# RWKV's last tile: the output projection in the scan's stage, its products behind the last scan step

## The reference, cut to what matters

```python
def rwkv_out(y, p, kvec, lnx, w_o):
    r, k, v, g = p["r"], p["k"], p["v"], p["g"]
    y = head_layernorm(from_heads(y), lnx[0], lnx[1], RW_HEADS, r.dtype)
    bonus = jnp.sum((r * k * kvec[2]).reshape(bn, L, RW_HEADS, RW_HEAD), axis=-1, keepdims=True) * v.reshape(...)
    return ((y + bonus.reshape(bn, L, D)) * g) @ w_o
...
        xl = xl + mod_l[2] * rmsnorm(yl, norm_g[layer, 1])          # yl is rwkv_out of the latents
        hl = modulate(rmsnorm(xl, norm_g[layer, 2]), mod_l[3], mod_l[4])
        xl = xl + mod_l[5] * rmsnorm(conv_ffn(hl, ...), norm_g[layer, 3])
```

## Time and profile before

| | us |
|---|---|
| median of 3 executions | 3187.83 (3187.26 to 3189.34) |
| the profiled execution | 3187.58 |
| its span, first to last instruction | 3185.6 |
| PE busy | 3038.0 (95%) |
| DVE busy | 1141.0 (36%) |
| ACT busy | 586.1 (18%) |

### The profile page before, as it was taken

How to read it: one execution, slowest core, us unless ns; L and a number is a source line. 1 busy time by engine, 2 the same in 40 slices (tenths; PEclk the granted TensorE clock), 3 DMA queues, 4 the chain that set the end, 5 groups by cost and what they waited for, 6 DMA issues and landing times. The chain is left out here.

```text
span 3185.6 us, 54300 instructions
## 1 busy us (share of the span) xinstructions
PE 3038.0 (95%) x24038; PEld 1843.0 (58%) x24038; DVE 1141.0 (36%) x2357; ACT 586.1 (18%) x1323; POOL 231.7 (7%) x202
## 2 busy tenths in 40 slices
PE   7999999899999999989987999999999799998998
PEld 5899884633333333344666544444464688887887
DVE  3455006301100111034055444431141778874650
ACT  1011013300000000022045110000021455542000
POOL 0000000100000000000022100000000233230000
PEclk9999999899999999989988999999999899998999
DMA  9846538589998899942000342333321100005440
GB/s 379 315 173 228 202 140 362 223 327 390 387 369 363 332 388 384 397 170 74 14 3 10 150 157 79 119 132 119 123 78 40 43 24 27 16 4 199 146 146 14
DMA packets 88492, 577.03 MB, mean 181 GB/s; under 512 B 9536, under 2 KB 15936, under 8 KB 20672
## 3 DMA queue, kind: packets, MB, share of 16 engines
q1 hardware_dynamic: 84800, 568.27, 45.9%
q10 hardware_dynamic: 3456, 5.24, 0.4%
HBM read 567.19 MB, written 6.29 MB: 180 GB/s over the span
## 5 line engine op out<-in xcount | busy, mean ns | idle before, releaser
L273 PE MATMUL ps<-H,ring 128*128 128x256 f32 (+1 forms) x2480 | 803.8, 486 | 12.6 <-PEq L3297 4.1
L273 PEld LDWEIGHTS ps<-H,ring 128*128 128x128 f32 x2480 | 477.9, 194 | 336.5 <-issue 296.3
L273 PE MATMUL ps<-W,ring 128*128 128x256 f32 (+1 forms) x1616 | 490.5, 465 | 9.1 <-DVE W L3144 4.1
L1963 PE MATMUL ps<-ring,W 128*32 128x512 f32 (+1 forms) x2816 | 461.4, 594 | 1.7 <-ACT H L2022 1.7
L273 PEld LDWEIGHTS ps<-W,ring 128*128 128x128 f32 x1616 | 307.1, 191 | 192.1 <-issue 166.8
L1963 PEld LDWEIGHTS ps<-ring,W 128*32 128x32 f32 (+1 forms) x2816 | 142.5, 123 | 306.6 <-issue 304.0
L1986 PE MATMUL ps<-ring,W 128*64 128x512 f32 (+1 forms) x1408 | 231.1, 594 | 0.0
L2253 DVE SCALAR_TENSOR_TENSOR W<-ps,vec,W 128x189 f32<-128x189 f32 (+3 forms) x396 | 173.2, 437 | 14.0
L1986 PEld LDWEIGHTS ps<-ring,W 128*64 128x64 f32 (+1 forms) x1408 | 70.9, 123 | 156.9 <-issue 156.9
L3728 POOL TENSOR_TENSOR ring<-ring 128x512 f32<-128x512 f32 x96 | 132.6, 1402 | 391.8 <-DVE ring L3761 310.1
L2071 DVE TENSOR_TENSOR H<-ps,H 128x256 f32<-128x256 f32 x66 | 28.0, 425 | 303.2 <-ACT H L2013 303.2
(11 more groups left out here) (468 smaller groups left out, 3172.9 us busy)
## 6 DMA issues: line engine op xcount, KB each, us to landing
ring<-weights SPq DMA_DIRECT2D x528, 1024.0 KB, 7.8
rkv<-W ACTq DMA_DIRECT2D x16, 256.0 KB, 2.0
ring<-rkv SPq DMA_DIRECT2D x8, 512.0 KB, 4.3
X<-tokens SPq DMA_DIRECT2D x2, 1024.0 KB, 9.2
rkv<-W ACTq DMA_DIRECT2D x8, 128.0 KB, 5.5
W<-rw_tiles SPq DMA_DIRECT2D x4, 256.0 KB, 2.7
ring<-rkv SPq DMA_DIRECT2D x8, 128.0 KB, 4.3
ring<-rw_tiles SPq DMA_DIRECT2D x4, 256.0 KB, 2.8
```

The source lines that it names most:

```text
L273: mm = pe.matmul(out(o), lhsT=k.ring[:, k.slot(at), p * P:(p + 1) * P], rhs=rhs(kk), start=kk == 0 and not (shared_bank and o % 2), stop=k ...
L1963: mm = pe.matmul(ps[at:at + n, r, :], lhsT=moe.Hg[:, kt, FIRST * e + first:FIRST * e + first + n], rhs=w[e][:, kk * WIDE:(kk + 1) * WIDE], ...
```

## The change

The output projection moves into the scan's stage. `stage_square` keeps its form for its other uses, with its DVE and ACT parts taken out into a class `Square`. In `stage_rwkv` the loop ends with j = 7 and the last tile's steps are written out behind it, for each engine:

- PE does the eight steps. `output_mean` and `output_squares` of tile 6 come behind steps 0 and 2 (the squares' sum came in step 6). Inside the steps there are places for products, with a count of 0. Behind `last_y`: the mean of tile 7, three products, the squares' sum of tile 7, the rest of the 36 products of outputs 0 to 5 with H tiles 0 to 5, the six with H tile 6, output 6 with tiles 0 to 6, outputs 0 to 6 with H tile 7, and output 7 with all. PE waits for `fin` and for the weight units as it comes to them. Two outputs share a PSUM bank; all eight stay in banks 2, 0, 1 and 3 until they are finished.
- ACT evicts outputs in the same order, each when both outputs of its bank are done.
- DVE does the gate and `finished_output(5)` ahead of the first state update, `output_difference(6)` behind the first, `finished_output(6)` behind the last, then tile 7's, and then the crosses.
- The sum of squares of tiles 6 and 7 goes to bank 7's second half, so step 4 waits for tile 6's root instead of its difference.
- POOL adds the squares at the end of its part of this stage.
- SP issues the first four units when tile 7's transposes, exponentials and query products are done, the other seven behind `wt_out` as before, and then the four refills. The scan's buffers in the ring are in another order, so that those used latest lie outside these four slots.

```diff
+class Square:
+    def vector(self, dve):
+        k = self.k
+        link = Link(k.dvel, dve)
+        for o in range(KD - 1):
+            dve.wait_ge(k.act.sem, k.act.at(o + 1))
+            self.rms.cross(dve, link, o, self.Y)
+        link.close()
+
+    def scalar(self, act, out, done=lambda o: o):
+        k = self.k
+        for o in range(8):
+            act.wait_ge(k.mm.sem, k.mm.at(self.out_done[done(o)]))
+            self.rms.square(act, o, out(o))
+            self.gate.out(act, self.Y, o, out(o)).then_inc(k.act.sem, 1)
...
+    squares_of = lambda q: ps[:, 2 if q < TILES - 2 else sc.Y, S:2 * S]
+    product = lambda o: ps[:, (2, 0, 1, 3)[o // 2], (o % 2) * S:(o % 2) * S + S]
...
-            sp.wait_ge(sem["wt_out"], 2 * TILES)
+            for name, n in (("tok", 6), ("exp", 8), ("vtok", 1), ("r", 1), ("gram_r", 1)):
+                sp.wait_ge(sem[name], n * TILES)
             for u in range(RING):
+                if u == U_SQ:
+                    sp.wait_ge(sem["wt_out"], 2 * TILES)
                 sp.dma_start(k.ring[:, k.slot(u), :], k.a["weights"][k.unit + u]).then_inc(k.w_in[k.slot(u)], 16)
+            refill(k, sp, square.unit_done, U_SQ)
...
-                        pe.wait_ge(sem["d"], s)
+                        pe.wait_ge(sem["d" if s < TILES - 1 else "root_d"], s)
...
-            for j in range(TILES + 2):
+            for j in range(TILES):
...
+            def products(places):
+                for o, kk in places:
+                    u, p = divmod(KD * o + kk, UT)
+                    if u not in landed:
+                        landed.add(u)
+                        pe.wait_ge(k.w_in[k.slot(u)], k.landed(u))
+                    if finished[0] <= kk:
+                        finished[0] = kk + 1
+                        pe.wait_ge(sem["fin"], kk + 1)
+                    mm = pe.matmul(product(o), lhsT=k.ring[:, k.slot(u), p * P:(p + 1) * P], rhs=k.H[:, kk, LAT],
+                                   start=kk == 0 and o % 2 == 0, stop=kk == last, skip_group_check=True)
+                    if kk == last:
+                        mm.then_inc(k.mm.sem, 1)
+
+            early = [(o, kk) for o in range(6) for kk in range(last - 1)]
+            for i in range(8):
+                step_a(last, i)
+                products(early[:0])
+                early = early[0:]
+                step_b(last, i)
+                if i == 0:
+                    output_mean(last - 1)
+                elif i == 2:
+                    output_squares(last - 1)
+                if i < 7:
+                    products(early[:0])
+                    early = early[0:]
+            last_y(last)
+            output_mean(last)
+            products(early[:3])
+            output_squares(last)
+            products(early[3:] + [(o, last - 1) for o in range(6)])
+            products([(6, kk) for kk in range(last)])
+            products([(o, last) for o in range(7)] + [(7, kk) for kk in range(KD)])
+            square.rms.add_totals(pe)
...
+            output(last - 1)
+            for i in range(8):
+                evict_sa(last, i)
+                if i == 1:
+                    output_squares(last - 1)
+                elif i == 2:
+                    output_roots(last - 1)
+            output(last)
+            output_squares(last)
+            output_roots(last)
+            square.scalar(act, product, lambda o: o | 1)
...
+            square.gate.vector(dve)
+            finished_output(last - 2)
+            for i in range(7):
+                next_state(last, i)
+                if i == 0:
+                    output_difference(last - 1)
+            finished_output(last - 1)
+            output_difference(last)
+            finished_output(last)
+            square.vector(dve)
```

More of the change, by code:

```diff
@@ L2132, in vector, with __init__, end @@
             dve, dve.value_load(self.moe.over[0:1, bass.ds(t, 1)], min_val=0, max_val=2 * NE - 1), self.gate))
+class Square:
+    def __init__(self, k, cols, Y, gate, rms):
+        self.k, self.cols, self.Y, self.gate, self.rms = k, cols, Y, gate, rms
+        self.n = cols.stop - cols.start
+        self.unit_done, self.out_done, self.signals, self.total = plan([i // KD for i in range(8 * KD)])
+    def vector(self, dve):
[11 more added lines that the diff above has]
+            self.gate.out(act, self.Y, o, out(o)).then_inc(k.act.sem, 1)
+    def end(self):
+        k = self.k
+        k.mm.base += self.total
+        k.act.base += 8
+        k.unit += U_SQ
 def stage_square(k, cols, Y, gate, rms):
     nc = k.nc
-    n = cols.stop - cols.start
-    unit_done, out_done, signals, total = plan([i // KD for i in range(8 * KD)])
+    square = Square(k, cols, Y, gate, rms)
+    out = lambda o: k.ps[:, o % 4, 0:square.n]
     with nc.Block() as block:
@@ L2168, in _ @@
         def _(act):
[L2169 to L2175, removed]
+            square.scalar(act, out)
+    square.end()
 def stage_conv_ffn(k, layer, cols, Y, ada, pre, rms, finish=None, ahead=True):
@@ L3709, in _ @@
                         decays(n, l - 4)
[L3710 to L3713, removed]
+                act.wait_ge(sem["wt"], j + 1)
+                for e in range(2):
+                    act.activation(sc.WT[j % 2][:, :, e, :], chunks8(ps[:, e, :]), ACT.Copy).then_inc(sem["wt_out"], 1)
+            last = TILES - 1
+            output(last - 1)
[9 more added lines that the diff above has]
+            square.scalar(act, product, lambda o: o | 1)
         @block.gpsimd
@@ L3729, in _ @@
                                            ALU.mult).then_inc(sem["ot"], 1)
+            square.rms.add(pool)
         @block.vector
@@ L3789, in decayed_b, with output_difference @@
                 dve.tensor_tensor(sc.BK[z], sc.ka2, flat(sc.eB[z]).unsqueeze(1).to_broadcast([P, 2, T]), ALU.mult).then_inc(sem["ab"], 1)
+            def output_difference(q):
+                dve.wait_ge(sem["mean"], q + 1)
+                if q:
+                    dve.wait_ge(sem["fin"], q)
+                dve.scalar_tensor_tensor(sc.d, ps[:, sc.Y, S:2 * S], -1.0 / CH, sc.y, ALU.mult, ALU.add).then_inc(sem["d"], 1)
             def finished_output(q):
@@ L3820, in _ @@
             dve.wait_ge(sem["masks_in"], 16)
-            for j in range(TILES + 3):
+            for j in range(TILES):
                 s, q, n = j - 1, j - 2, j + 1
-                here, ahead, behind = inside(j), inside(n), inside(q)
-                if here:
-                    masked_grams(j, 0)
+                ahead, behind = inside(n), inside(q)
+                masked_grams(j, 0)
                 next_state(s, 0)
[L3827 to L3838, removed]
-                next_state(s, 1)
[L3840 to L3845, removed]
@@ L3851, in _ @@
                 if behind:
-                    dve.wait_ge(sem["mean"], q + 1)
-                    if q:
-                        dve.wait_ge(sem["fin"], q)
-                    dve.scalar_tensor_tensor(sc.d, ps[:, sc.Y, S:2 * S], -1.0 / CH, sc.y, ALU.mult, ALU.add).then_inc(sem["d"], 1)
+                    output_difference(q)
                 for l in range(1, 6):
```

173 lines of the change are left out of this document (89 added, 84 removed).

## The result

| | before | changed |
|---|---|---|
| median of 20 executions, us | 3187.18 (3184.39 to 3189.34) | 3191.61 (3188.54 to 3198.17) |
| span of the profiled execution, us | 3185.6 | 3189.5 |

The ratio is 1.0015, 95% interval 1.0009 to 1.0021: 4.4 us slower, where 3.4 us faster than the profiled execution was forecast. The last product does come earlier, but by 7.3 us and not by 13.1, and the tail gives 9.8 back, as forecast.

A forecast was written before the change was run, and what follows sets the result against it. It saw PE busy for 95% of the span, with gains where PE waits or runs at its lower clock. Last product 13.1 us earlier, tail 9.7 lost: -3.4 from the profiled 3187.6, median 3184.4 us, range 3180.5 to 3188.5.

The forecast's parts named there:

- the tail: After the last product (E): outputs end together, crosses end at E + 8.3, next stage's first product at E + 17.2.
- turn 7: Tile 7's preparation beside tile 6's steps, up to the last tile's first state update: 0.1 us later, bounds 0 and 0.3.
- the steps' first update to the last: Last tile's scan steps: 1.95 us saved by DVE's new order, 2.5 by keeping the full clock.
- mean to first product: Last tile's norm: products ahead cover the 6.56 us chain, saving 5.7 us, bounds 4.5 and 6.1.
- first product to last, with the sum: Output projection: products start at full clock as PE no longer idles, saving 3.1 us, bounds 0 and 3.1.
- last product to the next stage's first: Behind the projection: E + 17.2 instead of E + 7.5, a loss of 9.7 us, bounds 6.4 and 11.6.
- the one on the weights: Weight units issued beside tile 7 and the scan steps cost PE 0 us, bounds 0 and 1.
- Two of the prediction's own signs: Right: state updates at most 2.1 us apart. Wrong: a stall in tile 7 beside the four early units.
- Its slowest rival: Clock falls in the steps and is still low when products start: 3190.0 us, 2.2 slower; chance 0.08.
- The clock: Steps 4 to 6 keep the full clock, 1.9 us a step, saving 2.5 us, bounds 0 and 3.0.
- one fall of the clock remains: Rival: the steps stay at low clock (2.5 us lost) or products begin at it (3.1); about 3187 us, chance 0.12.
- The products: Behind the last step: first product within 0.6 us of the mean, `fin` ready or nearly so, 64 products in 28 us.

The follow-up runs named there:

- e1: Changed kernel with the seven later weight units issued only behind the last scan step; 3187.24 us, ratio 1.0001 to the kernel before.
- e7: As e5, but all eleven weight units issued behind the last scan step; 3181.48 us, ratio 0.9985 to the kernel before.
- e8: Kernel before plus three added 1 MB transfers to the output tensor, beside tiles 2, 3 and 4; 3186.56 us, ratio 1.0002.
- e9: As e8, but the three added transfers are 0.875 MB each in rows of 7 KB, some 130 packets; 3187.28 us, ratio 0.9999.
- e5: e3's product order, one weight unit issued early beside tile 7 and ten behind the last scan step; 3175.28 us, ratio 0.9965 to the kernel before.
- e6: As e5, but the early weight unit comes in eight pieces of 128 KB; 3176.19 us, ratio 0.9966 to the kernel before.
- e3: Changed kernel with its weight transfers, but outputs 0 to 2 first, then 3 to 7 one after another, each in its own bank; 3180.68 us, ratio 0.9980.
- e2: As e1, and the first four weight units issued one by one, about 7 us apart; 3191.43 us, ratio 1.0014 to the kernel before.
- e12: The changed kernel once more, for a second profile; 3190.55 us, ratio 1.0009 to the kernel before.
- e4: e3's order of products with e2's weight transfers; 3179.82 us, ratio 0.9981 to the kernel before.
- e10: Changed kernel with its weight transfers, but no product before the last tile's norm is finished; 3197.35 us, ratio 1.0029 to the kernel before.
- e11: As e10, with the seven later weight units behind the last scan step; 3191.68 us, ratio 1.0012 to the kernel before.

## Why the prediction was wrong

The kernel came out slower where faster was forecast, and outside the range. The terms, in us from profile to profile (before, changed, forecast of the difference):

| term | before | changed | difference | forecast |
|---|---|---|---|---|
| turn 7 | 40.2 | 40.8 | +0.6 | +0.1 |
| the steps' first update to the last | 16.0 | 12.7 | -3.3 | -4.4 |
| last update to the mean | 2.8 | 5.1 | +2.3 | 0 |
| mean to first product | 6.6 | 0.9 | -5.7 | -6.1 |
| first product to last, with the sum | 30.8 | 29.5 | -1.3 | -2.7 |
| last product to the next stage's first | 7.5 | 17.3 | +9.8 | +9.7 |
| from there to the end | | | +1.4 | 0 |

**The step that failed** is the one on the weights: "so I charge 0 (bounds 0 and 1)". It looked at the earlier trace rows, where eleven units ran beside a step of 1.73 us, and took it that transfers cost PE nothing. That was step 2, within the first 4 us of the transfers. The packets of PE's code came as late in the kernel before, 9.3 and 7.0 us behind one another, and it did not run out, because it took only 284 and 291 records in these times: it waited 2.28 us for DVE and then ran at half the clock. The change took both the wait and the slow clock away. PE took 377 and 344 records in such times and stopped twice. So the gain of the clock and the cost of the transfers meet: the faster PE uses its instructions up. Taken out, the stops are worth 4.4 us (e1, give or take about 3.6 by the two intervals), with the 1.6 us of clock that follow them. That makes the kernel even with before, not faster.

What is then left of the forecast's 3.4 us can be read in e1's profile: steps, chain, products and tail differ from before by -4.4, 0.0, -6.0, -2.6 and +9.8 us, each within about 0.1 of the forecast. Turn 7 took 42.0 us there, 1.8 more than before, and the stretch behind the tail 1.4 more. Turn 7 varies between profiles: 39.2 to 42.4 us in the six with four units beside it, 40.0 to 40.2 in the four with nothing beside it (before, e7, e8, e9). The changed kernel's +0.6 lies within that scatter.

Two of the prediction's own signs spoke against it: state updates 3.00 us apart where at most 2.1 would be right, and stops in turn 7 beside the four early units. Its slowest rival, 3190.0, lies near the measured time by luck: it had the clock low through the steps, and the clock was full there.

**The clock.** Steps 4 to 6 at full clock: right in this kernel, and e1 shows 1.8 to 1.9 us a step, forecast 1.9. Step 3 took 2.16, forecast 1.93. Not right in e5 and e6, where the steps began at half of it; why is open. The fall at the products was priced by a rival ("one fall of the clock remains", 3.1 us) and came half as large, behind a stop that no rival had.

**The products.** Mean to first product 0.90 us, forecast 0.43; no wait for `fin` or a unit. As forecast.

**The tail.** E + 17.2 was forecast, E + 17.3 measured; the crosses ended at E + 8.4, forecast 8.3; the eight sums took 1.87, forecast 1.9. The seven crosses lost 2.8 us to POOL against the prediction's prices for them alone (10.4), forecast 2.7; that it hit so well inside its bounds of 1.1 and 4.4, from the one row of 0.62 us, is in part luck. e3 shows that the order of the products alone makes or mends the tail.

**The rest.** From the next stage's first product to the end it is 1.4 us more: behind a PE wait of 2.0 us at the start of the down projection, which both kernels have, the clock fell in the changed kernel and not before. It fell or not in kernels that are the same there (1.4 more in e1, e2, e3, e6, e7 and e12, not in e4, e5, e10 and e11), so it isn't one of the change's terms that I can price. It didn't fall in any of the three profiles of the old order (before, e8, e9), so whether the change makes it likelier is open.

**A version that beats both** came out of it: e5_one_early, 3175.28 us in 5 executions, 0.35% less than before (0.22% to 0.48%).

## What to carry to other kernels

PE's instructions share the DMA engines with the data. Beside code of many small matmuls a transfer of 1 MB or more can stop PE for 1 to 3 us, so put it beside few large ones: ten such units beside products of 256 columns stopped nothing (e5). Whether cutting it in pieces helps is shown by one profile only. When work is moved ahead, ask what its results were hidden beside: eight outputs that all end together cost 9.8 us, most of it DVE's crosses, and another order of the same 64 products gave it back. And a row read where an engine waits or runs slowly says nothing of the same place at full pace.

## What the runs showed of the hardware

- PE's code came in packets of 16 KB, each the code of 256 of its records: all 83 "issue" stops over 0.35 us lie at whole multiples of 256 records from one another (within 1), and PE started again 2.2 to 3.0 us behind a packet's start.
- Stops of 0.6 to 2.9 us came at the same two instructions in four profiles, beside DMA engines that were nearly full (0.90 and 0.99), and never there without them. With no large transfer near, stops at other packet ends reached 0.98 us (e11, at 2543.9).
- Four single units cost turn 7 6.7 and 6.5 us (e2 and e4, 46.9 and 46.7 us against 40.2). Four in one burst cost between -1.0 and 2.2 us in six profiles.
- DVE operations with two SBUF inputs took 0.99 us beside POOL's adds and 0.42 alone.
